# A two-layer hybrid block: the upward product of the feed-forward part on the unrated x, with the norm's rate multiplied in on GpSimd

## What is computed

```python
def rms_norm(x, g):
    y = xf * lax.rsqrt(jnp.mean(xf * xf, axis=-1, keepdims=True) + EPS)
    return (y * g).astype(x.dtype)

def conv_ffn(h, w_up, conv_w, conv_b, w_down):      # w_up [1024, 5632], w_down [2816, 1024]
    u = h @ w_up
    u = conv_b + sum(conv_w[j] * causal_shift(u, CONV_WIDTH - 1 - j) for j in range(CONV_WIDTH))
    gate, val = jnp.split(u, 2, axis=-1)
    return (jax.nn.silu(gate) * val) @ w_down

x = x + conv_ffn(rms_norm(x, norm_ffn_g[l]), ...)
```

## Time and profile before

| | us |
|---|---|
| median of 3 runs | 994.84 |
| the profiled execution | 994.69 |
| its span in the profile | 992.9 |
| TensorE busy | 971.7 |
| VectorE busy | 778.7 |
| ScalarE busy | 631.9 |
| GpSimd busy | 12.2 |

### The profile page before, as it was taken

The page is one execution under the profiler, slowest core; times in us unless marked ns, Lnnn a source line. Parts: engine busy times, 40 slices in busy tenths (PEclk is TensorE's granted clock), DMA queues, the critical chain, the costliest instruction groups (busy, mean ns, idle before and its releaser), DMA issues.

```text
span 992.9 us, 21221 instructions
## 1 busy us (share of the span) xinstructions
PE 971.7 (98%) x7846; PEld 862.2 (87%) x7846; DVE 778.7 (78%) x1242; ACT 631.9 (64%) x992; POOL 12.2 (1%) x33
## 2 busy tenths in 40 slices
PE   9999999999999999999999999999998999999997
PEld 8998987777689999999999989877776999998886
DVE  5899753996778998878778996459777779988886
ACT  6974525776836665766679444276866566666766
POOL 0000001000000000000000000010000000000000
PEclk9999999999999999999999999999999999999999
DMA  7463254344545565555534523543535446565554
GB/s 265 161 204 103 71 163 163 127 155 144 178 141 191 174 209 189 192 190 177 192 105 171 194 102 96 165 134 132 192 121 176 150 162 200 176 225 187 193 184 163
DMA packets 46388, 164.27 MB, mean 165 GB/s; under 512 B 5888, under 2 KB 6064, under 8 KB 46304
## 3 DMA queue, kind: packets, MB, share of 16 engines
q1 hardware_dynamic: 44496, 159.85, 47.8%
q10 hardware_dynamic: 1008, 1.89, 0.6%
q0 software_dynamic: 800, 1.33, 0.4%
HBM read 161.48 MB, written 1.05 MB: 164 GB/s over the span
## 4 chain that ended last, share of the span: by engine, by line
PE 75%; DVE 11%; ACT 8%; issue 4%; DMA 2%; ACTq 0%; SPq 0%; DVEq 0%
PE psum L494 74%; DVE sb_lo L1459 3%; ACT sb_rw L1035 2%; ACT sb_inv L1035 2%; ACT sb_hi L1035 2%; DMA sb_raw<-w_stream 2%; DVE sb_small L1778 1%; ACT L1323 1%; ACT L1035 1%; DVE sb_inv L1694 0%; DVE sb_inv L1673 0%; DVE sb_rw L1533 0%; DVE sb_inv L1634 0%; DVE sb_rw L1628 0%; DVE sb_inv L1760 0%
## 5 line engine op out<-in xcount | busy, mean ns | idle before, releaser
L1459 DVE TENSOR_TENSOR sb_lo<-sb_raw,sb_hi 128x1024 fp32r<-128x1024 f32 x296 | 356.5, 1220 | 65.8 <-ACT sb_hi L1035 63.9
L1035 ACT ACTIVATE sb_hi<-sb_raw 128x1024 fp32r<-128x1024 f32 (+1 forms) x298 | 309.4, 1051 | 120.6 <-PE psum L494 90.7
L494 PE MATMUL psum<-sb_hh,sb_hi 128*128 128x256 f32 x800 | 203.4, 289 | 1.1 <-DVE sb_hl L1466 1.1
L494 PE MATMUL psum<-sb_hl,sb_hi 128*128 128x256 f32 x800 | 199.7, 285 | 0.0
L494 PE MATMUL psum<-sb_o,sb_hi 128*128 128x256 f32 (+1 forms) x992 | 198.5, 326 | 0.0
L494 PEld LDWEIGHTS psum<-sb_o,sb_hi 128*128 128x128 f32 x992 | 159.4, 191 | 13.1
L494 PEld LDWEIGHTS psum<-sb_hh,sb_hi 128*128 128x128 f32 x800 | 154.6, 193 | 7.8 <-issue 3.7
L494 PEld LDWEIGHTS psum<-sb_hl,sb_hi 128*128 128x128 f32 x800 | 155.1, 194 | 0.3
L494 PE MATMUL psum<-sb_o,sb_lo 128*128 128x256 f32 x688 | 128.2, 283 | 0.0
L494 PE MATMUL psum<-sb_hh,sb_lo 128*128 128x256 f32 x800 | 121.3, 284 | 0.0
L494 PE MATMUL psum<-sb_hi,sb_o 128*128 128x512 f32 x368 | 106.0, 397 | 6.9 <-DVE sb_rw L1533 5.1
(11 more groups left out here) (193 smaller groups left out, 1086.8 us busy)
## 6 DMA issues: line engine op xcount, KB each, us to landing
sb_raw<-w_stream SPq DMA_DIRECT2D x299, 512.0 KB, 3.9
sb_pm<-mix_par ACTq DMA_DIRECT2D x2, 512.5 KB, 3.3
y_t<-sb_rw SPq DMA_DIRECT2D x3, 256.0 KB, 2.0
sb_pm<-mix_par SPq DMA_DIRECT2D x1, 512.5 KB, 10.2
sb_x<-x_t ACTq DMA_DIRECT2D x2, 256.0 KB, 4.5
sb_raw<-w_stream SPq DMA_DIRECT2D x2, 256.0 KB, 4.5
sb_x<-x_t SPq DMA_DIRECT2D x1, 512.0 KB, 6.7
sb_rw<-final_g POOLq DMA_DIRECT2D x1, 512.0 KB, 3.6
```

The lines of the kernel that those rows point to most:

```text
L494: return pe.matmul(out, lhsT, rhs, start=start, stop=stop, skip_group_check=True)
L1035: return act.activation(out, in_, func, scale=scale, bias=bias, **kw)
L1459: tt(lo[:, s, :], raw[:, s, :], hi[:, s, :].bitcast(F32), ALU.subtract).then_inc(lo_done, 1)
```

## The change

- All 22 tiles go wide, on the unrated x: `hh` and `hl` become the halves of one tensor `h2`, so that one matmul of 512 columns moves both. `RATED`, `XR`, `rate`, `rated_hi` and `rated_lo` go.
- ACT's `low_half` and DVE's `add_up` stand behind every tile; `scale_up` goes. For tiles 0 and 1 there is `first_low_half`, both of a tile ahead of its convs.
- GpSimd multiplies each sum (`UM`, 128x256, in SBUF) by the rate (`rs`), 44 instructions a layer. ACT's `conv` waits for it (`up_scaled`); PE's next use of the bank waits for DVE's add (`up_added`).
- The load of the last norm's weights (`GF`), a GpSimd DMA, moves from behind `rated_lo` to behind tile 0 of the last layer.
- Turn 0 is written out, and turns 1 to 4 are the hardware loop.

```diff
@@ gpsimd
-                if l == DEPTH - 1:
-                    pool.wait_ge(rated_l, 2 * DEPTH)
-                    pool.dma_start(GF[:, :], fin_in).then_inc(fin_loaded, 16)
+                pool.wait_ge(rms_inv, 2 * l + 2)
+                for t in range(FT):
+                    for which in range(2):
+                        k = 2 * (t % 2) + which
+                        pool.wait_ge(up_added, l * 2 * FT + 2 * t + which + 1)
+                        pool.tensor_tensor(UM[:, k, :], UM[:, k, :], rs[:, 0:T], ALU.mult).then_inc(up_scaled, 1)
+                    if t == 0 and l == DEPTH - 1:
+                        pool.dma_start(GF[:, :], fin_in).then_inc(fin_loaded, 16)
@@ tensor, two_slabs (tile 0)
+                        if wide:
+                            mm(bank[i][:, :], hi[:, s, cols], h2[:, :, k, :], k == 0, False)
+                            last = mm(bank[i][:, 0:T], lo[:, s, cols], hh[:, k, :], False, k == KT - 1)
@@ tensor, ffn_up
-                    if t >= RATED_FROM:
-                        for k, cols in tiles_k:
-                            mm(out[:, :], hi[:, s, cols], RATED[:, :, k, :], k == 0, False)
...
-                    else:
-                        for k, cols in tiles_k:
-                            hi_mm(out[:, 0:T], hi[:, s, cols], (hh[:, k, :], hl[:, k, :]), k == 0)
...
+                    for k, cols in tiles_k:
+                        mm(out[:, :], hi[:, s, cols], h2[:, :, k, :], k == 0, False)
+                    pe.wait_ge(lo_done, l * SLABS + n + which + 1)
+                    for k, cols in tiles_k:
+                        last = mm(out[:, 0:T], lo[:, s, cols], hh[:, k, :], False, k == KT - 1)
@@ scalar
+            def first_low_half(l, t, which):
+
+                act.wait_ge(slab_done, l * SLABS + FFN0 + 2 * t + which + 1)
+                do(UM[:, 2 * t + which, :], bank[2 * t + which][:, T:2 * T], ACT.Copy).then_inc(low_out, 1)
...
                 for t in range(2):
                     for which in range(2):
+                        first_low_half(l, t, which)
+                    for which in range(2):
                         conv(l, t, t, which, 8 + 4 * (2 * t + which), False)
                     ahead(l, FFN0 + 2 + t)
@@ vector
-            def scale_up(l, t, u, which, slab):
-                k = 2 * (u % 2) + which
-                dve.wait_ge(slab_done, slab + 1)
-                tt(UM[:, k, :], bank[k][:, 0:T], rs[:, 0:T], ALU.mult).then_inc(up_scaled, 1)
-
             def add_up(l, t, u, which):
                 k = 2 * (u % 2) + which
...
+                dve.wait_ge(low_out, l * 2 * FT + 2 * t + (which + 1))
+                tt(UM[:, k, :], UM[:, k, :], bank[k][:, 0:T], ALU.add).then_inc(up_added, 1)
```

More of the change, by code:

```diff
@@ L547, in dense, with two_slabs @@
                 last.then_inc(slab_done, 1)
-            def two_slabs(slab, s0_, tiles):
+            def two_slabs(slab, s0_, tiles, wide):
                 pe.wait_ge(lo_done, slab + 2)
@@ L555, in two_slabs @@
                         s, cols = (s0_ + i) % RING, slice(k * P, (k + 1) * P)
-                        last = split_mm(bank[i][:, 0:T], (hi[:, s, cols], lo[:, s, cols]),
-                                        (hh[:, k, :], hl[:, k, :]), k == 0, k == KT - 1)
+                        if wide:
+                            mm(bank[i][:, :], hi[:, s, cols], h2[:, :, k, :], k == 0, False)
+                            last = mm(bank[i][:, 0:T], lo[:, s, cols], hh[:, k, :], False, k == KT - 1)
+                        else:
+                            last = split_mm(bank[i][:, 0:T], (hi[:, s, cols], lo[:, s, cols]),
+                                            (hh[:, k, :], hl[:, k, :]), k == 0, k == KT - 1)
                         if k == KT - 1:
@@ L937, in ffn_up @@
                     if t > 1:
-                        pe.wait_ge(up_scaled, l * 2 * FT + 2 * t + which - 3)
+                        pe.wait_ge(up_added, l * 2 * FT + 2 * t + which - 3)
                     tiles_k = [(k, slice(k * P, (k + 1) * P)) for k in range(KT)]
-                    if t >= RATED_FROM:
-                        for k, cols in tiles_k:
-                            mm(out[:, :], hi[:, s, cols], RATED[:, :, k, :], k == 0, False)
-                        pe.wait_ge(lo_done, l * SLABS + n + which + 1)
-                        for k, cols in tiles_k:
-                            last = mm(out[:, 0:T], lo[:, s, cols], RATED[:, 0, k, :], False, k == KT - 1)
-                    else:
-                        for k, cols in tiles_k:
-                            hi_mm(out[:, 0:T], hi[:, s, cols], (hh[:, k, :], hl[:, k, :]), k == 0)
-                        pe.wait_ge(lo_done, l * SLABS + n + which + 1)
-                        for k, cols in tiles_k:
-                            last = mm(out[:, 0:T], lo[:, s, cols], hh[:, k, :], False, k == KT - 1)
+                    for k, cols in tiles_k:
[3 more added lines that the diff above has]
+                        last = mm(out[:, 0:T], lo[:, s, cols], hh[:, k, :], False, k == KT - 1)
                     last.then_inc(slab_done, 1)
@@ L1337, in low_half @@
                 do(UM[:, k, :], bank[k][:, T:2 * T], ACT.Copy).then_inc(low_out, 1)
[L1339 to L1342, removed]
             def silu(l, t, u):
@@ L1398, in turn @@
                             silu(l, t, u + r)
-                            if rated and r == 0:
+                            if r == 0:
                                 low_half(l, i, u + 1, 0)
@@ L1402, in turn @@
                             product(l, t, u + r)
[L1404 to L1407, removed]
+                turn(0)
+                with act.Fori(1, FTURNS) as i:
+                    turn(i)
                 if l + 1 < DEPTH:
@@ L1872, in _ @@
                 ahead(l, FFN0 + 1)
-                dve.wait_ge(rms_inv, 2 * l + 2)
                 for t in range(2):
                     for which in range(2):
-                        scale_up(l, t, t, which, l * SLABS + FFN0 + 2 * t + which)
+                        add_up(l, t, t, which)
                     for which in range(2):
@@ L1900, in turn @@
                             t, col = FU * i + (u + r), 8 * FU * i + (8 + 8 * (u + r))
-                            slab = l * SLABS + 3 * FU * i + (o + 2 * r)
-                            up(t, u + r, 0, slab)
+                            add_up(l, t, u + r, 0)
                             if r == 0:
@@ L1908, in turn @@
                             conv(l, t, u + r, 0, col)
-                            up(t, u + r, 1, slab + 1)
+                            add_up(l, t, u + r, 1)
                             take(o + 2 + 2 * r)
@@ L1912, in turn @@
                             product(l, t, u + r)
-                            if not rated:
-                                piece(i, u, r)
                         take(o + 5)
                         product_lo(l, FU * i + (u + 1), u + 1)
[L1918 to L1935, removed]
+                turn(0)
+                with dve.Fori(1, FTURNS) as i:
+                    turn(i)
                 assert own.n - before == DVE_OWN["turn"], ("dve turn", own.n - before)
```

45 lines of the change are left out of this document (9 added, 36 removed).

## The result

The changed kernel takes 1073.38 us (four runs, 1072.69 to 1074.87) against 994.76 us for the kernel before in the same comparison: a ratio of 1.0791, with a 95% interval of 1.0772 to 1.0810. That is 78.6 us more, where 51 were forecast. The direction and the engine that becomes the bound were right; the time lies outside the stated range.

What follows compares the result with a forecast made beforehand. PE was taken to bound the kernel, then DVE: pairs add 22.7 us in layer 0 and 26.0 in layer 1, tiles 0 and 1 2.3 net, +51.0 on 994.69, say 1046 us. Own range 1022 to 1062; 8-in-10 range 993.5 to 1060.

Steps and rivals of the forecast that it cites:

- What bounds, and that DVE takes over: Feed-forward pairs: PE bounds at 16.94 us; DVE, with 14.7 us of work, becomes the bound when 2.2 us are added.
- The wide form saves 0.085 us a slab: Upward slabs on PE: 2.88 us narrow, 2.795 us wide; 3.1 us off the path over both layers, at most 3.4.
- GpSimd can't read beside the split: After each add in steady pairs: GpSimd's product starts only when DVE's split ends; DVE waits 1.25 us a sum; chance 0.45.
- The rival of free reads: GpSimd's product runs beside DVE's split in the pairs, PE stays the bound: 994.6 us, 992.4 to 997; chance 0.33.
- the shared case: GpSimd's product and DVE's split run together, both stretched: about 1.0 us a pair, 1017 us, 997 to 1022; chance 0.22.
- The product's size: One GpSimd product of 256 elements, estimated from memset rows: 0.62 us, between 0.32 and 0.72 us.
- The bounds' slope: Each 0.1 us of product length is worth 8 us in all: 0.32 us gives 1022 us, 0.72 us gives 1054.
- A pair of 19.35 us: Steady pair on DVE: 14.7 us of need plus 4.65 us of waiting for product and conv, against PE's 16.94 us.
- the handovers around product and conv: In DVE's wait for each upward sum: 0.03 us beside 0.62 us of product and 0.60 us of conv.
- 14.7 us of DVE: DVE's work in a wide pair of the kernel before: 16.94 us less 2.24 us of idle gaps, small gaps included.
- Tiles 0 and 1: Start of each layer's feed-forward part: later convs delay ACT's splits, PE stands 1.5 us a layer; 2.3 us net in all.
- PE's gap at +6: Sign: PE waits 1 to 2 us at slab +6 in either layer, 1.1 us in the sum, whichever case holds.

Runs made afterwards that it cites:

- the last kernel: Against the kernel before: product by the rate on DVE, turns written out, tiles 0 and 1 narrow with fused scaling, other tiles wide; 991.99 us, ratio 0.9968.

## Why the prediction was right and wrong, step by step

- **What bounds, and that DVE takes over.** Right. DVE did no more work and became the bound by waiting, four times a pair, ended by ACT's conv.
- **The wide form saves 0.085 us a slab.** Right: 36 slabs less two waits of 0.19 us are 2.7 us, measured 2.5 us in the feed-forward parts of the kernel without the product, and 32 slabs are 2.7 us, measured 2.7 us in the last kernel. In whole times only the second is clear of zero.
- **GpSimd can't read beside the split.** This was the choice on which the forecast stood, with no row of before for it. Shown in three ways: a write in its place runs beside the split at full length, the product falls to 0.74 us when the split is moved away, and one input is kept out as two are. The rival of free reads fell by that; the shared case fell because no split grew beyond 1.23 us. The rule of the Trainium skill (SBUF — State Buffer, Who interferes with whom) holds in its first half, DVE first and GpSimd waiting for DVE's instruction, to within the 0.1 us by which a blocked product is shorter than a fresh one. In its second half, GpSimd first, DVE was held 0.20 us by an instruction of 0.84 us, not for the whole of it.
- **The product's size.** Taken at 0.62 us from the memset rows, upper end 0.72; alone it takes 0.73 us and behind a split 0.60. That the value used fits the place is luck: nothing in the memset rows says what a read costs, or that a blocked product is shorter. In tiles 0 and 1, where DVE is idle, it is the upper end that fits. The bounds' slope, 8 us for each 0.1 us, held: half the columns took off 24.4 us.
- **A pair of 19.35 us: the step that failed.** The prediction put the handovers around product and conv at 0.03 us in all and said of the loop that it changes "nothing either, turns 2 to 4 are that now". They are 0.03 + 0.04 us written out and 0.18 + 0.15 us in the loop, and sixteen of the twenty pairs are in the loop. Turns 2 to 4 were in a loop before too, but beside a bound PE, where it costs nothing; the forecast itself had just moved the bound. The loop's form was worth 22.8 us, and the range had room for 0.1 us of handover, 8 us. Where the turns are written out, the wait was forecast well (1.27 us against 1.25), and a pair is 18.8 us: the sum was 0.5 us high there, because its 14.7 us of DVE come from a pair in the loop, in which the step from tap to tap is 0.63 us instead of 0.52, four times. In the loop a pair is 20.3 us. All pairs together were forecast at 48.7 us and cost 61.7.
- **Tiles 0 and 1.** The place was right: PE waits for the split of slab +6, 1.50 us against 1.1. The size was low, 5.0 us in both layers against 2.3.
- **The ends of the layers.** Missing, 10.5 us against nothing. No term of the sum had the last downward slabs wait. In the kernel before `product_lo` of the last tile is done 2.6 us (layer 0) and 0.7 us (layer 1) ahead of its slab; now DVE's chain comes late and PE waits 4.72 and 6.22 us for it, with a downward slab still to do. With sums of pairs alone this can't be seen: when the bound moves to another engine, the last thing that the old one needs from the new one has to be followed as well.
- **The whole.** 51.0 us forecast, 80.2 measured in the spans: 13.0 more in the pairs, 2.7 in tiles 0 and 1, 10.5 at the ends, 3.0 in parts that the change doesn't touch. Written out, the changed kernel lies inside the range, at 1050.57 us, but by luck in good part: its pairs cost some 38 us, 11 less than forecast, and the ends 10 more.
- **What would show it.** Of the signs named, seen: DVE idle for 1.26 us (written out) to 1.53 us ahead of the first tap, three times a pair and shorter the fourth time, behind a held `product_lo`; pairs of 18.8 to 20.3 us; PE's gap at +6. Not seen as named: products that start when a split ends. Their records start 0.08 us behind the add, which the prediction listed as a sign of being wrong; it is their ends that lie behind the split. The gaps of PE are ended more by ACT's split (20.7 us in layer 0's feed-forward part) than by DVE's (1.8 us), and stand ahead of upward slabs, since ACT's splits stand behind convs that wait for GpSimd.

## What to carry to other kernels

Before a step goes to GpSimd because GpSimd is idle, look at what DVE does at that moment: beside a DVE instruction with both inputs in SBUF a GpSimd instruction that reads makes no headway, and if DVE's next work hangs on it, both durations lie on the path one after the other. Here the same step cost 76 us more on the idle engine than on the busy one. And when a forecast moves the bound to another engine, price again what was hidden under the old one: the handovers inside a hardware loop, and the last result that the old bound waits for.

## What the runs showed of the hardware

- A one-input multiplication by a constant took GpSimd 0.84 us for 128x256 fp32, a two-input product 0.72 to 0.75 us, a two-input product of 128 columns 0.45 us at the least, a memset of 256 columns 0.31 us. The one-input instruction was not the cheaper one.
- GpSimd's record contains the time in which it is kept out: it begins 0.1 us behind the add and ends 0.60 us behind the split, 1.65 us in all. A mean of 1572 ns in the page's group is no duration of work.
- Behind PE's gaps of 4.72 us in layer 0 and of 6.22 us in layer 1 the last downward slab began at the lower of the clock's two levels (1.2 GHz). In layer 1, from matmul to matmul of 512 columns it is 0.43 us (1061.91 to 1062.34); at the full clock it is 0.23 us, from the earlier trace rows: 2.795 us of a wide slab less eight steps of 0.12, over eight. One stretch of layer 0 and the two at the end of layer 1, with the granted clock in the third column from the right (0.50, 0.50, then 0.96):

```profile
533.00:536.00 3.00, 2.99 (x14) 3.00 (x15) 1.86 (x3) 1.57 (x3) 0.00 (x0) 0.50 0.64 201
...
1061.00:1066.00 5.00, 4.65 (x11) 3.72 (x12) 0.53 (x3) 2.36 (x7) 0.00 (x0) 0.50 0.03 11
1066.00:1069.00 3.00, 1.98 (x8) 1.25 (x7) 2.18 (x5) 1.43 (x5) 0.00 (x0) 0.96 0.47 175
```

  In layer 1 eleven matmuls at 0.43 instead of 0.23 us are 2.2 us. In layer 0 eighteen matmuls of 256 columns take 4.0 us (533.01 to 536.99) instead of 2.2. Both long waits were paid a second time in the slab behind them.
